# Six small SBUF tiles allocated ahead of the large ones, with a pad between, in a two-block float32 kernel

## The reference

```python
# block 1, once
proj = rms_norm(x, g) @ w_in                       # 2048 -> 18432
hr   = rg_lru(rnn_x, ...)                          # conv, gates, scan
y_rnn  = (hr * silu(rnn_gate)) @ w_rnn_out
y_attn = (o * silu(attn_gate)) @ w_attn_out        # 3 dilated groups of 8 heads
y = (sigmoid(g_rnn) * y_rnn + sigmoid(g_attn) * y_attn) @ w_o
x = x + rms_norm(y, ln_post_g)
# block 2, for l in range(2)
u = rms_norm(x, g_pre[l]) @ w_in[l]                # 2048 -> 16192
y = sum(gate[n] * ((o_n * silu(z_n)) @ w_branch[l, n]) for n in 3)   # MLA, differential, chunk-band attention
x = x + y @ w_out[l]
```

## Time and profile before

| | |
|---|---|
| median of 3 executions | 3156.31 us (3156.0 to 3157.43) |
| profiled execution, first to last instruction (span) | 3154.9 us; its own time isn't listed, the median less the span is 1.4 us |
| busy: TensorE / weight loads / VectorE / ScalarE | 99% / 87% / 68% / 55% of the span |
| time that packets took, share of 16 DMA engines | 58.9% |
| granted TensorE clock, mean | 0.998 |

### The profile page before, as it was taken

How to read it: one execution, slowest core, us unless ns; L and a number is a source line. 1 busy time by engine, 2 the same in 40 slices (tenths; PEclk the granted TensorE clock), 3 DMA queues, 4 the chain that set the end, 5 groups by cost and what they waited for, 6 DMA issues and landing times.

```text
span 3154.9 us, 52176 instructions
## 1 busy us (share of the span) xinstructions
PE 3134.1 (99%) x18230; PEld 2741.8 (87%) x18230; DVE 2130.5 (68%) x2741; ACT 1733.0 (55%) x2291; POOL 0.2 (0%) x4
## 2 busy tenths in 40 slices
PE   9999999999999999999999999999999999999999
PEld 7888888888888788888888888888888888888888
DVE  7677575666667687766666555777776666655575
ACT  5685444444445556656555555645665656555563
POOL 0000000000000000000000000000000000000000
PEclk9999999999999999999999999999999999999999
DMA  7656655555556555565556655566556565665555
GB/s 230 194 168 200 198 187 166 183 177 172 181 167 208 178 168 163 156 198 173 174 171 192 184 181 182 181 198 186 158 157 202 170 179 167 192 189 180 178 185 175
DMA packets 569809, 571.67 MB, mean 181 GB/s; under 512 B 26352, under 2 KB 565488, under 8 KB 569712
## 3 DMA queue, kind: packets, MB, share of 16 engines
q1 hardware_dynamic: 569712, 570.42, 58.9%
HBM read 568.25 MB, written 2.10 MB: 181 GB/s over the span
## 4 chain that ended last, share of the span: by engine, by line
PE 97%; DVE 1%; ACT 1%; DMA 0%; SPq 0%; issue 0%; ACTq 0%; DVEq 0%
PE pg L537 91%; PE pa L771 1%; PE pa L788 1%; PE pa L537 1%; PE pa L778 1%; PE pa L747 1%; PE pa L789 1%; DVE hl L1276 0%; PE pa L704 0%; DMA raw<-w_o 0%; PE pa L878 0%; DMA raw<-w_in 0%; ACT hl L933 0%; SPq L456 0%; DVE uT L1357 0%
## 5 line engine op out<-in xcount | busy, mean ns | idle before, releaser
L537 PE MATMUL pg<-hT,hl 128*128 128x512 f32 x11456 | 2030.6, 337 | 1.1 <-DVE hl L1276 1.1
L537 PEld LDWEIGHTS pg<-hT,hl 128*128 128x128 f32 x11456 | 1750.9, 188 | 261.1 <-DVE hl L1276 4.2
L1276 DVE TENSOR_TENSOR hl<-raw,hl 128x1024 fp32r<-128x1024 f32 (+1 forms) x1071 | 1256.0, 1209 | 314.5 <-ACT hl L933 306.8
L933 ACT ACTIVATE hl<-raw 128x1024 fp32r<-128x1024 f32 (+1 forms) x1071 | 1084.0, 1044 | 313.1 <-PE pg L537 293.8
L537 PE MATMUL pg<-uT,hl 128*128 128x256 f32 (+1 forms) x3712 | 639.1, 333 | 15.9 <-DVE uT L1357 7.5
L537 PEld LDWEIGHTS pg<-uT,hl 128*128 128x128 f32 x3712 | 558.4, 190 | 92.2 <-issue 14.2
L941 ACT ACTIVATE corr<-pg 128x512 f32<-128x512 f32 x286 | 170.3, 596 | 843.0 <-PE pg L537 843.0
L537 PE MATMUL pg<-hl,hT 128*128 128x256 f32 (+1 forms) x1792 | 317.9, 336 | 0.0
L1283 DVE TENSOR_TENSOR work<-pg,corr 128x512 f32<-128x512 f32 (+1 forms) x154 | 105.8, 687 | 303.7 <-ACT corr L941 303.5
L537 PEld LDWEIGHTS pg<-hl,hT 128*128 128x128 f32 x1792 | 274.9, 188 | 40.7
L1283 DVE TENSOR_TENSOR gat<-pg,corr 128x512 f32 (+1 forms) x71 | 48.9, 689 | 139.4 <-ACT corr L941 139.4
(11 more groups left out here) (191 smaller groups left out, 1369.2 us busy)
## 6 DMA issues: line engine op xcount, KB each, us to landing
raw<-w_in SPq DMA_DIRECT2D x791, 512.0 KB, 4.7
raw<-w_br SPq DMA_DIRECT2D x96, 512.0 KB, 4.3
raw<-w_out SPq DMA_DIRECT2D x64, 512.0 KB, 4.7
raw<-w_rnn SPq DMA_DIRECT2D x32, 512.0 KB, 4.8
raw<-w_o SPq DMA_DIRECT2D x32, 512.0 KB, 5.0
raw<-w_att SPq DMA_DIRECT2D x16, 512.0 KB, 4.4
raw<-w_uq SPq DMA_DIRECT2D x16, 384.0 KB, 4.0
tab<-tabs SPq DMA_DIRECT2D x5, 896.0 KB, 7.2
```

The costliest lines, as they stand in the source:

```text
L537: return nc.tensor.matmul(out, lhsT, rhs, start=start, stop=stop, skip_group_check=True)
L933: nc.scalar.activation(hl4[:, j % 2, 0, a:a + n], raw[:, bass.ds(j % 2 * UC + a, n)], ACT.Copy)\
L1276: tt(hl4[:, j % 2, 1, a:a + n], raw[:, bass.ds(j % 2 * UC + a, n)], hl4[:, j % 2, 0, a:a + n].bitcast(F32), ALU.subtract).then_inc(lo_done, 1)
```

## The change

The six small tiles (`corr`, `cst`, `tab`, `v1`, `v2`, `sm`) are allocated first, then a pad of 464 float32 (1856 bytes) that nothing reads or writes, then the large tiles in their former order, and `work` last. Every large tile then starts at a multiple of 16 KB. No instruction is added, removed or moved on any engine or queue; only the SBUF addresses in them differ.

```diff
 T_C, T_S, T_R, T_M, N_TAB = 0, 256, 512, 640, 640 + 1152
+PAD = 464
 T_RG = T_M + 384
...
+        corr = sb("corr", 2 * 512)
+        cst = sb("cst", 3 * P)
+        tab = sb("tab", N_TAB)
+        v1 = sb("v1", N_V1)
+        v2 = sb("v2", N_V2)
+        sm = sb("sm", 200)
+
+        sb("pad", PAD)
         raw = sb("raw", 2 * UC)
         hl = sb("hl", 4 * UC, F32R)
         hT = sb("hT", NT * 512, F32R)
...
         mix = sb("mix", NT * S)
         gat = sb("gat", NT * S)
-        corr = sb("corr", 2 * 512)
-        cst = sb("cst", 3 * P)
-        tab = sb("tab", N_TAB)
-        v1 = sb("v1", N_V1)
-        v2 = sb("v2", N_V2)
-        sm = sb("sm", 200)
         work = sb("work", 31 * 256 + 128)
```

## The result

The changed kernel takes 3172.67 us (median of 4 executions, 3172.45 to 3173.84) against 3156.33 us before (4 executions): the ratio is 1.005, 95% interval 1.0038 to 1.0062. It lost 16.3 us; forecast was no difference.

A forecast was written before the change was run, and what follows sets the result against it. TensorE was taken to bound the kernel, by matmul pace and 17.1 us of waits. Span 3154.9 + 0 + 0 + 0 - 0.3 = 3154.6 us, plus 1.4 us for the median of runs: 3156.0 us, range 3152 to 3160 us.

The forecast's parts named there:

- The bound: Whole kernel: TensorE busy 3134.1 of 3154.9 us, so only matmul pace or its 17.1 us of waits can move the time.
- the matmul reads: Term for TensorE's operand reads at the new addresses: taken as 0, with bounds of -221 and +221 us.
- 216 ns: Time read for each float32 matmul of 256 columns: 512 column times (213.3) and a rest of 3 ns.
- -221 and +221 us: Bounds of the matmul-read term: the whole unexplained rest of the wide matmuls goes, or the same 8% comes once more.
- The pace rival: Matmul pace falls with aligned starts: 2935 us if the whole rest goes, 3145 us for a twentieth; chance 4%.
- 26.7 ns: Part of each 346.7 ns wide and narrow matmul pair, 8%, not explained by its 768 columns (320.0 ns).
- The neighbourhood rival: `hl` unit 1 and half of `hT` share 32 KB, VectorE's writes slow TensorE's reads: 26 us more, 3182 us; chance 3%.
- VectorE, ScalarE: Term for both engines' work at shifted tile offsets: 0, as offsets are worth 3 ns at most and both have slack.
- The cover: TensorE hides VectorE and ScalarE unless the splits of weights grew by more than about a third.
- DMA: Term for load packets with aligned destinations: 0 to -1 us, 0.3 us in the sum.
- the transfer rival: The chain's 13.2 us of transfers lose a ninth, 1.5 us: 3154.8 us; chance 25%, 1% for over 6.3 us.

The follow-up runs named there:

- p1: A kernel of its own without the reference: 18 streams of 64 wide and narrow fp32r pairs at varied tile distances; 346.7 to 353.4 ns a pair over ten distances.
- l2: The kernel before with 1920 bytes of pad in front, so every large tile starts at a multiple of 2048; 3156.59 us, ratio 0.9999.
- l3: The changed kernel with 128 bytes more of pad and 64 ahead of `work`, giving the low address bits of before; 3157.2 us, ratio 0.9999.

## Why the prediction was wrong

- **The bound** was read rightly: TensorE's pace or its 17.1 us of waits, nothing else. The waits came out at 17.8 us, so all but 0.7 us of the loss is pace.
- **The step that failed** is that of the matmul reads: "I take 0, since every row that varies the place or the neighbours shows the pace unmoved." The runs showed in its place a second rhythm, 353.3 ns a pair instead of 346.7, that 5719 matmuls fell into instead of 247, for 17.8 us. The rows that I held against it looked at one rhythm at different moments: all of them were from streams that had locked into 346.7 ns. The step before it failed too: "If from two operands or two engines meeting in one piece of the memory, the pace had to vary with who else is at work" doesn't follow for two operands of TensorE itself, whose distance was the same in all those rows, and the row of two operands in one tile compared mean durations, whose ends are modelled, and not starts. The bounds of the step, -221 and +221 us, did hold the truth, +16; my range dropped them. The trace of before had the sign of a second pace, 22.63 us for 128 matmuls at 1166 us, in the view that I read for the earlier trace rows; I took three equal rows from it and didn't ask about the unequal one. "What stays is a fixed cost by the low bits of the start address alone" named the wrong quantity: it is the distance between tiles.
- **A misread row**: the 216 ns of the earlier trace rows are not one float32 matmul. In p1 12 float32 matmuls leave 24 rows 216 ns apart, so a matmul of 256 columns leaves two. The rest of 3 ns is that of a row.
- **The pace rival** (aligned starts are faster) falls by l2, aligned at 3156.59 us. The reasoning that some of the 26.7 ns answers to addresses was right; what was found is a step of 6.7 ns, and only to the worse: no alternating stream of any run was faster than 346.7 ns a pair.
- **The neighbourhood rival** had the right sign and the wrong mechanism: l3 lies in the same pieces as the changed kernel and takes 3157.2 us. That writers in the same 32 KB cost nothing, no run contradicts.
- **VectorE, ScalarE**: 0, as forecast. The split is 1221 and 1053 ns, the addition 689 to 691 ns after, as in the earlier trace rows. The cover was put too small: with 32% of the span idle, some 1010 us, the 1240.5 us of splits could grow by four fifths on average, not by a third.
- **DMA**: the queue's share is 58.6% with aligned destinations against 58.9%, in a span 0.5% longer. Per packet that is 52.2 ns both times. By the reading of the Trainium skill (DMA: Bandwidth & Descriptors, How a descriptor splits into AXI transactions) for writes it would have been some 52% (the prediction has 53), an estimate from that page: nothing of it shows on the destination side here. The 1.5 us of the transfer rival aren't there.

## What to carry to other kernels

A pace that is exact to the nanosecond isn't proof that nothing touches it: a stream of matmuls can lock into one of several rhythms (346.7 or 353.3 ns a pair here), and pads, or a few matmuls in another order ahead of it, can pick another. In a kernel at 99% TensorE, list all paces per instruction in the chain, not only the commonest, before costing a change of addresses at nothing, and keep the distances modulo 256 bytes between tiles that matmuls read when adding or moving a tile. At two distances between stationary and moving operand (96 and 224 bytes, alternating fp32r pairs) five beginnings each led into the fast rhythm and none into the slow one. At 224 the rest of the layout lost most of its influence; at 96 grouped orders and exchanged sides took back nearly half of the gain.

## What the runs showed that I hadn't expected

- The pace of 64 alternating pairs depends on the distance between stationary and moving tile modulo 256: from 346.7 to 353.4 ns a pair in ten distances.
- Narrow matmuls alone are faster at 64 bytes (113.3 ns) than at 0 (120.0), wide ones slower (233.3 against 226.7).
- The Trainium skill (SBUF — State Buffer, Who interferes with whom) gives TensorE two read ports, one for the moving operand and one for the weights, and lets only the shared pair of VectorE and GpSimd cause contention. With it, nothing here should depend on a distance between tiles; the runs show that it does, and they decide. That moving reads and weight loads meet in one piece of the memory is the nearest explanation, but no run shows a meeting: why the distances act as they do, and what the last 26.7 ns of each pair are, stays open. So does how the matmuls that read `work` and the small tiles change the first two steps of a stream: p1's lead-in, with both operands from one tile, didn't reproduce it.
